# Column tiles of 32 for the samples' attention products and for the query-state product of their matrix memory

## What is computed

```
s = jnp.einsum('bqhd,bshd->bhqs', qb.astype(jnp.float32), k) * DH_F ** -0.5
s = s + jnp.swapaxes(cq, 1, 2)[..., :, None] - jnp.swapaxes(ck, 1, 2)[..., None, :]
s = jnp.where(k_pos[None, :] <= q_pos[:, None], s, -jnp.inf)
p = jax.nn.softmax(s, axis=-1)
return jnp.einsum('bhqs,bshd->bqhd', p, v).astype(qb.dtype)
```

```
num = wg[..., None] * jnp.einsum('blhd,bhde->bhle', qc, C) + jnp.einsum('bhls,bshe->bhle', qk, vc)
```

## Time and profile before

| what | value |
|---|---|
| median of 3 runs | 5133.01 us |
| lowest, highest | 5125.77, 5140.24 us |
| span of the profiled execution | 5137.4 us |
| TensorE matmuls, busy | 4489.3 us, 16494 |
| TensorE weight loads, busy | 2746.5 us |
| VectorE busy | 3085.4 us |
| ScalarE busy | 953.6 us |
| GpSimd busy | 1252.6 us |

### The profile page before, as it was taken

How to read it: one execution, slowest core, us unless ns; L and a number is a source line. 1 busy time by engine, 2 the same in 40 slices (tenths; PEclk the granted TensorE clock), 3 DMA queues, 4 the chain that set the end, 5 groups by cost and what they waited for, 6 DMA issues and landing times. The chain is left out here.

```text
span 5137.4 us, 47634 instructions
## 1 busy us (share of the span) xinstructions
PE 4489.3 (87%) x16494; PEld 2746.5 (53%) x16494; DVE 3085.4 (60%) x6265; ACT 953.6 (19%) x1784; POOL 1252.6 (24%) x970
## 2 busy tenths in 40 slices
PE   8996698885999996888887898836999999999989
PEld 5555454553555554666664565635555455454534
DVE  1003322067766665888884366787777777777742
ACT  1113111110011101555542112112000000000023
POOL 0000022001444442333330000000544444444410
PEclk9998788997999998777877999979999999999999
DMA  4433452963999998888776777445999999999951
GB/s 165 144 127 100 158 195 92 357 231 144 422 381 388 394 378 291 314 300 306 297 289 249 287 288 260 172 164 193 416 418 419 416 418 415 414 414 413 414 208 57
DMA packets 338721, 1477.65 MB, mean 288 GB/s; under 512 B 38146, under 2 KB 153650, under 8 KB 217938
## 3 DMA queue, kind: packets, MB, share of 16 engines
q0 software_dynamic: 119872, 824.76, 39.9%
q1 hardware_dynamic: 218642, 650.30, 34.2%
HBM read 1369.00 MB, written 115.38 MB: 289 GB/s over the span
## 5 line engine op out<-in xcount | busy, mean ns | idle before, releaser
L2287 POOL DMA_INDIRECT ex_uv<-in_uv,idx x768 | 1161.5, 1512 | 1936.8 <-DVE ex_acc L2344 1688.4
L2328 DVE CUSTOM_DVE_ANT_0 ex_uv<-ex_uv,ex_xp 128x1024 f32<-128x1024 f32 x768 | 913.8, 1221 | 313.4 <-DMA ex_uv<-in_uv,idx 274.7
L2344 DVE SCALAR_TENSOR_TENSOR ex_acc<-ex_uv,ex_wt,ex_acc 128x1024 f32<-128x1024 f32 x768 | 943.1, 1281 | 10.0 <-DVE C L880 3.2
L384 PE MATMUL proj_psum_acc<-proj_w,aT_later 128*128 128x385 f32 x2304 | 749.0, 487 | 63.2 <-DMA proj_w<-in_w_in 63.2
L2634 PE MATMUL exp_psum_dn<-exp_dn_big,exp_dn_gg 128*128 128x512 f32 x1536 | 689.6, 599 | 24.1 <-DVE exp_dn_gg L2556 24.1
L2625 PE MATMUL exp_psum_dn<-exp_dn_xT,exp_dn_big 128*128 128x384 f32 x2048 | 683.5, 487 | 14.1 <-DMA exp_dn_big<-in_ud 14.1
L384 PEld LDWEIGHTS proj_psum_acc<-proj_w,aT_later 128*128 128x128 f32 x2304 | 437.1, 190 | 374.7 <-DMA proj_w<-in_w_in 63.4
L2625 PEld LDWEIGHTS exp_psum_dn<-exp_dn_xT,exp_dn_big 128*128 128x128 f32 x2048 | 390.2, 191 | 313.9 <-issue 61.9
L2634 PEld LDWEIGHTS exp_psum_dn<-exp_dn_big,exp_dn_gg 128*128 128x128 f32 x1536 | 293.3, 192 | 375.8 <-issue 347.4
L296 PE MATMUL proj_psum_acc<-proj_w,aT 128*128 128x385 f32 x1152 | 378.1, 489 | 5.1 <-DMA proj_w<-in_w_in 3.3
L1956 PE MATMUL rt_psum_b<-rt_w,rt_yT 128*128 128x512 f32 x576 | 270.4, 633 | 50.3 <-ACT rt_yT L2022 42.4
(11 more groups left out here) (374 smaller groups left out, 4448.4 us busy)
## 6 DMA issues: line engine op xcount, KB each, us to landing
proj_w<-in_w_in SPq DMA_DIRECT2D x48, 1540.0 KB
rt_w<-in_w_q SPq DMA_DIRECT2D x36, 2048.0 KB, 8.0
exp_dn_big<-in_ud SPq DMA_DIRECT2D x128, 512.0 KB
exp_dn_big<-in_vd SPq DMA_DIRECT2D x128, 512.0 KB, 8.0
scratch_z<-proj_zs SPq DMA_DIRECT2D x216, 192.5 KB, 1.9
rt_w<-in_w_br_m SPq DMA_DIRECT2D x18, 2048.0 KB, 9.8
rt_w<-in_w_br_f SPq DMA_DIRECT2D x18, 2048.0 KB
rt_w<-in_w_out SPq DMA_DIRECT2D x18, 2048.0 KB, 8.1
```

Source lines behind the costliest of these rows:

```text
L384: mm = pe.matmul(acc[j % SLOTS][:, 0:CW], aT[:, k, t * P:(t + 1) * P], w[:, u % U, k, :], start=(k == 0), stop=(k == KD - 1))
L2287: pool.indirect_dma_start(self.uv[:, slot, :], None, self.uv_tab, bass.IndirectOffsetOnAxis(ap=self.idx[:, at:at + 1], axis=0)).then_inc(s ...
L2328: dve.tensor_tensor_reduce(self.uv[:, slot, 0:D], self.uv[:, slot, 0:D], self.xp[:], 1.0, 0.0, ALU.mult, ALU.add, self.dot[:, g % 2, j:j + ...
L2344: dve.scalar_tensor_tensor(out=self.acc[:, j % 2, :], in0=self.uv[:, slot, D:2 * D], scalar=self.wt[:, g % 2, j:j + 1], in1=self.acc[:, j ...
```

## The change

A matmul whose result lies on 32 partitions, beginning at partition 0, 32, 64 or 96, has a column tile of the array to itself. The change writes three groups of products in this form.

- Scores: pair `p` writes its own 32 partitions. The weights shrink to the pair's 32 columns. Both groups of pairs, cached and new, come first, then the matmuls that span the whole result. `start=True` now stands on each pair's first matmul.
- Mix: each 128 positions take 4 matmuls, one for each pair, of 32 probability columns against the pair's own 128 value columns, so 16 in place of 4, and 4 in place of 1 for the new positions. The result shrinks from 128 x 512 to 128 x 128, and with it VectorE's scaling.
- Query-state product: samples go in pairs `g`, each on its 32 partitions; the weights for sample `2 g + e` are 32 columns of which 16 are zero. There are 16 matmuls of 257 columns as before. VectorE fills the weights in two copies in place of one.

The two memsets of the weights shrink from 128 x 2048 to 128 x 512. The diff, cut to its core:

```diff
@@ FoxSample @@
+    PAIR = 2 * DSEQ
-        self.kn, self.qd = st.sb("skn", [P, 2, KD, DSEQ]), st.sb("sqd", [P, 2, 2, 4, P])
+        self.kn, self.qd = st.sb("skn", [P, 2, KD, DSEQ]), st.sb("sqd", [P, 2, 2, 4, 2 * DSEQ])
-        self.y = st.sb("sy", [P, 2, 512])
+        self.y = st.sb("sy", [P, 2, 2 * DF])
...
-                           self.y[h * DSEQ:(h + 1) * DSEQ, f, h * DF:(h + 1) * DF]).then_inc(self.y_out[f], 16)
+                           self.y[h * DSEQ:(h + 1) * DSEQ, f, h % 2 * DF:(h % 2 + 1) * DF]).then_inc(self.y_out[f], 16)
...
         for p in range(4):
-            pe.matmul(old, self.qd[:, b, f, p, :], self.kc[:, b, 4 * f + p, :], start=(p == 0), stop=False)
+            at = slice(self.PAIR * p, self.PAIR * (p + 1))
+            pe.matmul(old[at], self.qd[:, b, f, p, :], self.kc[:, b, 4 * f + p, :], start=True, stop=False)
+        for p in range(4):
+            at = slice(self.PAIR * p, self.PAIR * (p + 1))
+            pe.matmul(new[at], self.qd[:, b, f, p, :], self.kn[:, b, 4 * f + p, :], start=True, stop=False)
         pe.matmul(old, sel, self.ck[:, b, 0:PAST], start=False, stop=True)
-        for p in range(4):
-            pe.matmul(new, self.qd[:, b, f, p, :], self.kn[:, b, 4 * f + p, :], start=(p == 0), stop=False)
...
+        W = 2 * DF
         for c in range(self.ST):
-            pe.matmul(self.y_ps[:], self.probT[:, c * P:(c + 1) * P], self.vc[:, b, c, f * 512:(f + 1) * 512],
-                      start=(c == 0), stop=False)
-        pe.matmul(self.y_ps[:], self.probT[0:DSEQ, self.ST * P:(self.ST + 1) * P], self.vn[:, b, f * 512:(f + 1) * 512],
-                  start=False, stop=True).then_inc(self.mixed, 1)
+            for p in range(4):
+                at, cols = slice(self.PAIR * p, self.PAIR * (p + 1)), slice(f * 512 + p * W, f * 512 + (p + 1) * W)
+                pe.matmul(self.y_ps[at, 0:W], self.probT[:, c * P + at.start:c * P + at.stop], self.vc[:, b, c, cols],
+                          start=(c == 0), stop=False)
+        for p in range(4):
...
+            mm = pe.matmul(self.y_ps[at, 0:W], self.probT[0:DSEQ, self.ST * P + at.start:self.ST * P + at.stop],
+                           self.vn[:, b, cols], start=False, stop=True)
+        mm.then_inc(self.mixed, 1)
...
-        dve.tensor_scalar(self.y[:, f, :], self.y_ps[:], self.inv[:, f:f + 1], None, ALU.mult).then_inc(self.y_ready, 1)
+        dve.tensor_scalar(self.y[:, f, :], self.y_ps[:, 0:2 * DF], self.inv[:, f:f + 1], None, ALU.mult
+                          ).then_inc(self.y_ready, 1)
@@ MlstmSample @@
-        self.qd = st.sb("nqd", [P, 2, N * P])
+        self.qd = st.sb("nqd", [P, 2, N // 2, 2, 2 * DSEQ])
...
-            for s in range(N):
-                for j in range(2):
-                    mm = pe.matmul(b[:, 0:DA], self.qd[:, j, s * P:(s + 1) * P], self.C[:, i % 2, s, j, :],
-                                   start=(s + j == 0), stop=(s == N - 1 and j == 1))
+            for j in range(2):
+                for e in range(2):
+                    for g in range(N // 2):
+                        mm = pe.matmul(b[2 * DSEQ * g:2 * DSEQ * (g + 1), 0:DA], self.qd[:, j, g, e, :],
+                                       self.C[:, i % 2, 2 * g + e, j, :], start=(j + e == 0), stop=(j + e == 2))
...
-            dve.tensor_copy(diag8(self.qd), self.qT[:].rearrange("p j (n t) -> p j n t", n=N)).then_inc(self.placed, 1)
+            halves = self.qT[:].rearrange("p j (g e t) -> p j g e t", e=2, t=DSEQ)
+            for e in range(2):
+                dve.tensor_copy(self.qd[:, :, :, e, e * DSEQ:(e + 1) * DSEQ], halves[:, :, :, e, :]
+                                ).then_inc(self.placed, 1)
```

More of the change, by code:

```diff
@@ L1292, in dve_place @@
             for e in range(2):
-                flat = self.qd[e * DF:(e + 1) * DF, b, f, :, :].rearrange("p c m -> p (c m)")
-                dve.tensor_copy(diag4(flat, e * DSEQ), self.qT[e * DF:(e + 1) * DF, 4 * f:4 * f + 4, t]
-                                ).then_inc(self.placed, 1)
+                dve.tensor_copy(self.qd[e * DF:(e + 1) * DF, b, f, :, e * DSEQ:(e + 1) * DSEQ],
+                                self.qT[e * DF:(e + 1) * DF, 4 * f:4 * f + 4, t]).then_inc(self.placed, 1)
         dve.tensor_copy(self.kn[:, b], self.kT[:, :, t]).then_inc(self.placed, 1)
@@ L1491, in pe_slot @@
             b = self.claim(pe, n)
-            pe.wait_ge(self.placed, i + 1)
+            pe.wait_ge(self.placed, 2 * i + 2)
             pe.wait_ge(self.c_in[i % 2], (i // 2 + 1) * N * 16)
             pe.wait_ge(self.c_cols, i * 2 + 1)
-            for s in range(N):
-                for j in range(2):
-                    mm = pe.matmul(b[:, 0:DA], self.qd[:, j, s * P:(s + 1) * P], self.C[:, i % 2, s, j, :],
-                                   start=(s + j == 0), stop=(s == N - 1 and j == 1))
+            for j in range(2):
[3 more added lines that the diff above has]
+                                       self.C[:, i % 2, 2 * g + e, j, :], start=(j + e == 0), stop=(j + e == 2))
             done(mm, n)
@@ L1637, in act_slot @@
             if i >= 1:
-                act.wait_ge(self.placed, i)
+                act.wait_ge(self.placed, 2 * i)
                 self.wait_full(act, self.group(i - 1, "s"))
@@ L1674, in act_slot @@
             act.sem_inc(self.free[n % self.BANKS], 1)
-def diag8(qd):
-    v = qd[:]
-    return bass.AP(tensor=v.tensor, offset=v.offset,
-                   ap=[v.ap[0], [NSEQ * P, 2], [P + DSEQ, NSEQ], [1, DSEQ]])
-def diag4(flat, first):
-    step = P + 2 * DSEQ
-    v = flat[:, first:first + 3 * step + DSEQ]
-    return bass.AP(tensor=v.tensor, offset=v.offset, ap=[v.ap[0], [step, 4], [1, DSEQ]])
 def stage_sample(nc, K, z, gates, T):
```

## The result

The changed kernel takes 5005.52 us (median of 4 runs, 4993.65 to 5007.87), the kernel before, beside it, 5130.88 us (median of 4 runs). The ratio on record is 0.9747 (the two medians alone give 0.9756), with a 95% interval of 0.9733 to 0.9762, that is 122 to 137 us.

A forecast was written before the change was run, and what follows sets the result against it. TensorE was taken to bound the samples' stage. Steps 51, query-state product 10, memset 1.3, weight copies -0.4 and scaling 0.4 sum to 62 us; less 8 given back, 54: 5137.4 to 5083 us, range 5025 to 5140.

The forecast's parts named there:

- What bounds the kernel: Samples' stage: TensorE is the bound, with a matmul in flight for 287.6 of 309.6 us; about 22 us are waits.
- How much overlaps: Rewritten products: matmuls start in program order, only neighbours on different tiles overlap; a call costs one matmul's time plus 0.03 us.
- The couples 0.46 and 0.14 us apart: Trace sign that the forecast is right: starts of lines 1251 and 1281 in couples, less than 0.05 us within a couple.
- the first rival: Rewritten products: all four column tiles run at once, giving 5032 us; chance 0.13.
- The forecast's 6.1 us of a step: Four rewritten score and mix phases of a step: 6.1 us for 9.3, saving 51 us in 16 steps.
- The rival's upper bounds: Step phases if all four tiles overlap: cached mix 1.2, new mix 0.45, cached scores 1.0, new scores 0.3 us.
- The bound of 0.03 us for a narrow load: Weight loads with 96 columns fewer: about 0.03 us each in place of 0.112, the pace where loads limit the mix.
- The query-state product: Its 32 instructions a head: 4.1 us plus 0.4 for form changes, from 6.9; 10 us saved in 4 heads.
- The floor of 0.056 us for an entry of the queue: TensorE's queue: if no entry passes faster, mix and new keys gain nothing and 27 us are saved, 5110.
- Give back 8 us, for waits and the clock: Samples' stage: 8 us of the gain lost to exposed VectorE and ScalarE work, loads and the clock, chosen between 0 and 22.
- the third rival: Samples' stage: partly filled array keeps the granted clock low; no gain at mean 0.68, 5176 us at 0.6; chance 0.12.
- The small terms: Samples' stage: shorter memset saves 1.3 us, VectorE's scaling 0.4; the 13 us before the next stage stay.

The follow-up runs named there:

- e5: Changed kernel with all calls of one column tile issued in a row, in mix, scores and query-state product: 5027.98 us, ratio 0.9786 to the kernel before.
- e9: Changed kernel with the cached mix issuing two calls of a tile in a row, twice for each tile: 5005.44 us, ratio 0.9747 to the kernel before.
- e11: Changed kernel with the cached mix issuing three calls of a tile in a row, then one call: 5016.7 us, ratio 0.9765 to the kernel before.
- e3: Kernel before with only the query-state product in column tiles: 5121.21 us, ratio 0.9965 to the kernel before.
- e8: Changed kernel with the prompt attention's mix also split into four column tiles: 4977.19 us, ratio 0.9686 to the kernel before.
- e4: Changed kernel with mix and query-state product all written to one column tile, partitions 0 to 31: 5084.3 us, ratio 0.9891 to the kernel before.
- e7: Changed kernel with the operands of 16 rows padded with zeros to 128 rows: 5000.06 us, ratio 0.9729 to the kernel before.

## Why the prediction was wrong

- **What bounds the kernel:** right. TensorE bound the stage, and 131.4 us came out of its stretch between first scores and last mix. In the measure of the earlier trace rows, up to the last DMA issue, it takes 178 us, where about 255 were forecast.
- **"How much overlaps":** this step failed. It read the order of the starts in the rows of before as a rule of the queue, and concluded that only "every other border overlaps", since a call's second matmul has to wait for its first and everything behind it would stand. Every matmul in those rows was on the same tile as its neighbour, so they could not show otherwise. The changed kernel shows the waiting matmul passed by those of the other tiles, and `e5`, `e9` and `e11` show how far: up to four to a tile. The couples 0.46 and 0.14 us apart, the sign of the forecast, aren't there; four starts within a pace, the sign of the first rival, are. That rival had 0.13. The step carries most of the miss: at full clock the four phases gave (9.30 - 2.41) x 16 = 110 us where 51 stood in the sum, and the query-state product 20 where 10 stood.
- **The sizes.** The forecast's 6.1 us of a step measured 2.41. The rival's upper bounds were themselves too high, in each of the four: 1.01 for 1.2, 0.36 for 0.45, 0.88 for 1.0, 0.16 for 0.3. They add up to 2.95, not to the 3.1 that the prediction used. So even the rival's 5032 was 27 us too high. The bound of 0.03 us for a narrow load came out near the truth with a wrong make-up: a load of 32 columns takes as long as one of 64, 0.11 (106/109/154 ns least, median and greatest at line 1251), but the loads of four tiles run side by side.
- **The query-state product:** 10 us forecast, 18 measured alone (`e3`), 20.4 less busy; the rival's bound of 4.9 a head, 19.6, was right. Here the same step failed.
- **The floor of 0.056 us for an entry of the queue:** refuted. 64 entries, 32 loads and 32 matmuls, pass in 1.01 us, 0.016 each.
- **Give back 8 us, for waits and the clock:** the two came out with opposite signs. TensorE's idle time in the stretch rose by 6.3 us, 4.5 of them the one wait on the load of `smp_nv`. The forecast had taken the loads, at an expected 185 GB/s, to be far from their limit; they ran at 270. The chain through VectorE and ScalarE, which was expected to show in a few steps, made no new wait. The clock cost less than before (next point), so on balance nothing was given back.
- **The clock:** the granted clock of the stretch fell from 0.89 to 0.84, the direction of the third rival, short of its point of 0.68 and above the 0.8 that was to show it. But a lower mean over a shorter stretch isn't a higher cost. Busy time times clock is 256 of 287.6 us before and 126 of 150 after, so the low level cost some 32 us before and 24 after, an estimate from these rows. It fell on other work: the heads of the query-state product had 0.76 to 0.89 before and 0.50 to 0.67 after.
- **The small terms:** the memset took 0.48 us (0.44 forecast), VectorE's scaling 0.351 (0.3), and the 13 us between the last issue and the next stage's first load stayed 13.1 (748.66 to 761.75).

```profile
568.63 0.48 DVE L1290 MEMSET smp_sqd<- 128x512 f32 x1 [24.24 <-DMA smp_nm_all<-in_m]
```

The prediction weighed the Trainium skill in two places. The Trainium skill, TensorE: Matmul & The Clock Gate, section Part 3: Packing small matmuls — row/col tiling, gives 2.38x for three column tiles, and says that matmuls start and end in program order. Here four tiles gave 4.1x for the cached scores (3.63 and 0.88) and 3.6x for the mix, which is more for each tile than the page's figure. The order of the starts doesn't hold across column tiles for these float32 calls, and the prediction had taken it as backing. The Trainium skill, TensorEngine Tiling (Array Packing), section Performance Considerations, warned of dimensions that are already small; the new keys' 16 columns gained the largest factor of all, 0.99 to 0.16.

## What to carry to other kernels

Where a product fills its weights with zeros, or computes blocks that nobody reads, write it in column tiles and alternate between the tiles in the program: four narrow calls then cost about what one costs. Even a full product can gain where few columns stream and the weight load sets its pace (`e8`, 64 columns), as far as other engines have time left. And a row can only bound what its instructions could have done: an order seen on one tile says nothing on two.

## What the runs showed of the hardware

- Matmuls on different column tiles pass each other; those of one tile run one after the other (32 of 128 columns in 3.61 us, `e4`). Four tiles start within 0.05 us and each keeps its pace of 0.11 us for 128 columns and 0.43 for 512 (two to a tile in 0.88 us, four in 1.77).
- The behaviour of `e5`, `e9` and `e11` is that of a short queue for each tile with room for four matmuls, one running and three waiting, filled in program order, where a full one stops all behind it. It gave 1.7 us ahead of the run that measured 1.74. It is a model that fits four orders (2.3 us for the 2.39 of `e5`), not something seen directly.
- 32 loads of 32 columns and 32 matmuls pass in 1.01 us. The number of instructions is not the limit at that pace, nor in the prompt's stage, where `e8` adds 3456 matmuls and the time falls.
- A change between 128 and 16 rows of weights costs about 0.1 us in the open in three places where `e7` takes it away (0.11, 0.14 and 0.08), and nothing that shows in a fourth.
- A load of 32 columns takes 0.109 us (median of line 1251), about as long as one of 64 (0.112); eight loads of line 1281 are in flight at once at 658.56 us.
